# The differential-attention stage: diagonals on ScalarE, and a new order of TensorE's and VectorE's work

## What is computed

```python
def diff_attention(q, k, v, lam, lam_init, subln_g):
    # 4 heads, two maps each, head dimension 64
        s = jnp.einsum('bqhmd,bkhmd->bhmqk', q_blk, k) * scale
        s = jnp.where(mask, s, NEG_INF)
        p = jax.nn.softmax(s, axis=-1)
        att = p[:, :, 0] - lam * p[:, :, 1]
        return jnp.einsum('bhqk,bkhe->bqhe', att, v)
    ...
    o = rms_norm(o, subln_g) * (1.0 - lam_init)
```

## Time and profile before

| | |
|---|---|
| median of 3 runs | 3535.96 us (3531.65 to 3537.88) |
| the profiled execution | 3533.43 us, of which the span is 3531.3 us |
| TensorE matmul busy | 2925.1 us, 83% of the span |
| VectorE busy | 2493.0 us, 71% |
| GpSimd busy | 1844.8 us, 52% |
| ScalarE busy | 843.0 us, 24% |
| granted TensorE clock, mean | 0.943 |
| moved by DMA | 1295.97 MB, 367 GB/s over the span |

### The profile page before, as it was taken

One profiled execution on the slowest core, in us unless ns is written; L12 is line 12 of the kernel. 1 busy time (PEld: TensorE's weight loads), 2 busy tenths in 40 slices (PEclk: granted clock), 3 DMA queues, 4 the chain that ended last, 5 costly groups with the idle time before them and its releaser, 6 DMA issues.

```text
span 3531.3 us, 33020 instructions
## 1 busy us (share of the span) xinstructions
PE 2925.1 (83%) x10296; PEld 1862.3 (53%) x10296; DVE 2493.0 (71%) x5300; ACT 843.0 (24%) x2407; POOL 1844.8 (52%) x1508
## 2 busy tenths in 40 slices
PE   8999688798799878787689878888789878877777
PEld 6677444366587534355477534356478444422222
DVE  1421567787887886888888876788797887754545
ACT  2320122222210122322210123322220123332223
POOL 0000144686677534577676634587577634554554
PEclk9999899999899989998799989999799999999999
DMA  4334499999999999999999999999999999999997
GB/s 163 111 108 154 152 419 420 414 368 395 335 392 409 408 401 417 421 407 409 364 398 409 409 387 409 421 382 394 360 361 409 409 417 418 416 421 422 421 421 331
DMA packets 281580, 1295.97 MB, mean 367 GB/s; under 512 B 31808, under 2 KB 32064, under 8 KB 211776
## 3 DMA queue, kind: packets, MB, share of 16 engines
q0 software_dynamic: 216576, 1073.84, 75.7%
q1 hardware_dynamic: 64544, 218.99, 16.5%
q10 hardware_dynamic: 288, 1.05, 0.1%
HBM read 1291.65 MB, written 2.10 MB: 366 GB/s over the span
## 4 chain that ended last, share of the span: by engine, by line
PE 47%; DMA 24%; DVE 13%; POOL 7%; issue 6%; ACT 3%; DVEq 0%; SPq 0%; POOLq 0%; ACTq 0%
PE bank L594 20%; DMA ring<-in_peer,eidx 18%; PE bank L847 11%; DMA work<-in_peer,eidx 6%; POOL ring L1192 5%; PE bank L798 5%; DVE ring L1225 3%; PE bank L809 3%; DVE acc L1230 2%; PE bank L669 2%; PE bank L645 1%; POOL ring L1187 1%; ACT dg L943 1%; PE bank L624 1%; PE bank L648 1%
## 5 line engine op out<-in xcount | busy, mean ns | idle before, releaser
L1225 DVE CUSTOM_DVE_ANT_0 ring<-ring,hp 128x1024 f32<-128x1024 f32 x816 | 984.0, 1221 | 303.3 <-DMA ring<-in_peer,eidx 302.4
L1192 POOL DMA_INDIRECT ring<-in_peer,eidx x808 | 986.8, 1221 | 398.0 <-issue 221.8
L847 PE MATMUL bank<-ring,dg 128*128 128x512 f32 x1784 | 837.0, 617 | 261.7 <-ACT dg L943 231.2
L1187 POOL DMA_INDIRECT ring<-in_peer,eidx x390 | 480.5, 1232 | 920.2 <-DVE eidx L1331 423.8
L594 PE MATMUL bank<-xt,panel 128*128 128x256 f32 x4096 | 922.8, 383 | 19.8 <-ACT xt L949 5.7
L594 PEld LDWEIGHTS bank<-xt,panel 128*128 128x128 f32 x4096 | 783.6, 192 | 152.7 <-issue 30.8
L847 PEld LDWEIGHTS bank<-ring,dg 128*128 128x128 f32 x1784 | 336.5, 196 | 734.9 <-issue 697.7
L1230 DVE SCALAR_TENSOR_TENSOR acc<-ring,wgt,acc 128x1024 f32<-128x1024 f32 x326 | 415.7, 1286 | 24.8 <-DMA ring<-in_peer,eidx 21.9
L847 PE MATMUL bank<-work,dg 128*128 128x512 f32 x704 | 328.7, 610 | 106.7 <-ACT dg L943 100.5
L1225 DVE CUSTOM_DVE_ANT_0 work<-work,hp 128x1024 f32<-128x1024 f32 x208 | 252.6, 1222 | 121.6 <-DMA work<-in_peer,eidx 121.4
L1187 POOL DMA_INDIRECT work<-in_peer,eidx x154 | 195.5, 1269 | 232.9 <-PE bank L847 151.9
(11 more groups left out here) (180 smaller groups left out, 2467.8 us busy)
## 6 DMA issues: line engine op xcount, KB each, us to landing
panel<-in_panels SPq DMA_DIRECT2D x368, 512.0 KB, 6.8
ring<-in_peer,eidx POOLq DMA_INDIRECT x1198, 17.0
work<-in_rel_bias SPq DMA_DIRECT2D x16, 512.0 KB, 8.0
work<-in_peer,eidx POOLq DMA_INDIRECT x306, 22.0
gb<-in_ln_g SPq DMA_DIRECT2D x8, 512.0 KB, 8.4
gb<-in_ln_b SPq DMA_DIRECT2D x8, 512.0 KB, 10.5
panel<-in_keys SPq DMA_DIRECT2D x16, 256.0 KB, 6.4
work<-in_x SPq DMA_DIRECT2D x4, 512.0 KB, 4.6
```

Of the source, the lines that this page charges most:

```text
L847: ins = mm(pa[t * 2 + half][:, :], dg[:, i % DIAGS, :], v_row[:, half * 512:(half + 1) * 512], start=(n == group[0]), stop=(n == group[-1]))
L1187: pool.indirect_dma_start(slots(slot, 2), None, t_in["peer"], bass.IndirectOffsetOnAxis(ap=eidx[:, 0, t, c:c + 1], axis=0)).then_inc(row_i ...
L1192: pool.indirect_dma_start(slots(slot, 1), None, one_row, bass.IndirectOffsetOnAxis(ap=eidx[:, which, t, c:c + 1], axis=0)).then_inc(row_in ...
L1225: v.tensor_tensor_reduce(row, row, hp[:, t, :], 1.0, 0.0, ALU.mult, ALU.add, hid[:, t, c:c + 1]).then_inc(used, 1)
```

## The change

TensorE's order in C becomes, for each u: scores(u+1), project_qk(u+2), weigh(u), outputs(u), swap_qk(u+2).

VectorE's becomes: maxima(u), rope(u+1), the two rows of key 4, and `inverses(u)`: only the reciprocals, and for map 1 their product with minus lambda, counted by a new semaphore `c_inv`. The diagonals of C are built by ScalarE, in `weights_c(u)`: four copies of the identity with the inverse as scale. In ScalarE's queue weights_c(u) and then take_qk(u+2) stand ahead of take_weighed(u), and exponentials 2 and 3 of u+1 follow take_out(u) together. Stage A keeps its order and its diagonals on VectorE.

```diff
--- before.py
+++ after.py
@@ -435,6 +435,7 @@
         pair_wgt = sem("pair_wgt")
         smax = {k: sem(f"smax_{k}") for k in "AC"}
         dg_done = {k: sem(f"dg_done_{k}") for k in "AC"}
+        c_inv = sem("c_inv")
         rope_done = sem("rope_done")
         rms_dg = sem("rms_dg")
         lam_sums = sem("lam_sums")
@@ -755,12 +756,13 @@
                 scores("C", s, 0)
                 swap_qk(s, 1)
                 for u in range(UNITS):
-                    weigh("C", s, u)
                     if u + 1 < UNITS:
                         scores("C", s, u + 1)
+                    if u + 2 < UNITS:
+                        project_qk("C", s, u + 2)
+                    weigh("C", s, u)
                     outputs("C", s, u)
                     if u + 2 < UNITS:
-                        project_qk("C", s, u + 2)
                         swap_qk(s, u + 2)
                 pe.wait_ge(pt_ev["C"], fills_before(s, "C", UNITS))
                 pe.wait_ge(o_ev["C"], (s + 1) * UNITS)
@@ -980,6 +982,15 @@
                        accum_out=esum[:, u % 2, i:i + 1]).then_inc(e_done[kind], 1)
                     gelus((s, kind, u, i))
 
+            def weights_c(s, u):
+
+                n = s * UNITS + u
+                for m in range(2):
+                    act.wait_ge(c_inv, n * 2 + m + 1)
+                    for i in (2 * m, 2 * m + 1):
+                        fn(dg[:, u % 2 * 4 + i, :], ident, ACT.Copy, scale=rinv[:, u % 2, i:i + 1]
+                           ).then_inc(dg_done["C"], 1)
+
             def take_weighed(kind, s, u):
                 for f, (m, lo, hi) in enumerate(fills(s, kind)):
                     c = fills_before(s, kind, u) + f
@@ -1064,17 +1075,16 @@
                 take_v("C", s)
                 exps("C", s, 0)
                 for u in range(UNITS):
+                    weights_c(s, u)
+                    if u + 2 < UNITS:
+                        take_qk("C", s, u + 2)
                     take_weighed("C", s, u)
                     gelus((s, "C", u, 4))
                     if u + 1 < UNITS:
                         exps("C", s, u + 1, (0, 1))
                     take_out("C", s, u)
                     if u + 1 < UNITS:
-                        exps("C", s, u + 1, (2,))
-                    if u + 2 < UNITS:
-                        take_qk("C", s, u + 2)
-                    if u + 1 < UNITS:
-                        exps("C", s, u + 1, (3,))
+                        exps("C", s, u + 1, (2, 3))
                 act.wait_ge(o_ev["C"], (s + 1) * UNITS)
                 fn(oroot[:], osq[:], ACT.Sqrt, bias=cst[:, C_EPS2:C_EPS2 + 1], scale=1.0 / P).then_inc(rms_root, 1)
                 gelus((s, "R", 0, 0))
@@ -1507,19 +1517,28 @@
                                     ).then_inc(smax[kind], 1)
                     rows((s, kind, u, i))
 
-            def diagonals(kind, s, u):
+            def diagonals(s, u):
                 n = s * UNITS + u
                 for m in range(2):
-                    dve.wait_ge(e_done[kind], n * 4 + m * 2 + 2)
+                    dve.wait_ge(e_done["A"], n * 4 + m * 2 + 2)
                     v.reciprocal(rinv[:, u % 2, 2 * m:2 * m + 2], esum[:, u % 2, 2 * m:2 * m + 2]).then_inc(*own.one())
                     step()
                     for i in (2 * m, 2 * m + 1):
-                        if kind == "C" and m == 1:
-                            ts(dg[:, u % 2 * 4 + i, :], ident, rinv[:, u % 2, i:i + 1], small[:, 13:14],
-                               ALU.mult, ALU.mult).then_inc(dg_done[kind], 1)
-                        else:
-                            ts(dg[:, u % 2 * 4 + i, :], ident, rinv[:, u % 2, i:i + 1], None, ALU.mult
-                               ).then_inc(dg_done[kind], 1)
+                        ts(dg[:, u % 2 * 4 + i, :], ident, rinv[:, u % 2, i:i + 1], None, ALU.mult
+                           ).then_inc(dg_done["A"], 1)
+
+            def inverses(s, u):
+
+                n = s * UNITS + u
+                for m in range(2):
+                    part = rinv[:, u % 2, 2 * m:2 * m + 2]
+                    dve.wait_ge(e_done["C"], n * 4 + m * 2 + 2)
+                    ins = v.reciprocal(part, esum[:, u % 2, 2 * m:2 * m + 2])
+                    if m:
+                        ins.then_inc(*own.one())
+                        step()
+                        ins = ts(part, part, small[:, 13:14], None, ALU.mult)
+                    ins.then_inc(c_inv, 1)
 
             def attention_stage(kind, s):
                 if kind == "C":
@@ -1528,10 +1547,13 @@
                     rows((s, "A", -1, 0))
                 for u in range(UNITS):
                     maxima(kind, s, u)
-                    diagonals(kind, s, u)
-                    if kind == "C" and u + 1 < UNITS:
+                    if kind == "A":
+                        diagonals(s, u)
+                    elif u + 1 < UNITS:
                         rope(s, u + 1)
                     rows((s, kind, u, 4))
+                    if kind == "C":
+                        inverses(s, u)
 
             def rms(s):
                 rows((s, "R", 0, 0))
```

## The result

The changed kernel takes 3587.78 us (median of 5 runs, 3582.71 to 3590.06) against 3533.3 us for the kernel before (median of 5 runs by then): a ratio of 1.0152 with a 95% interval of 1.0134 to 1.017, 54 us slower. The forecast was 3556, with a range that ended at 3574. The direction was right and the size was not: 54 us instead of 20.

A forecast was written before the change was run, and what follows sets the result against it. Stage C was taken to be paced by TensorE with short waits. Its phases summed to +22.8 us, about +20 after what comes back, so 3553 for the profiled execution and 3556 for the median, range 3543 to 3574.

The forecast's parts named there:

- The waits: Full units of C: outputs waits 0.57 us for ScalarE's copy, swap 1.04 for take_out, scores 1.58 for the rotation.
- The table load ahead of the exponentials: Once per stage C in phases 1 to 3, after a gelu: +1.2 us in phase 2, +0.8 in 1 and 3.
- The sum without the clock: Stage C's changes without a clock fall in middle units: +4.9, +6.1, +5.7, +6.1 us by phase, together +22.8.
- the restart at the lower clock: Scores(1) of C in phases 1 and 3 runs slow after TensorE's long wait for VectorE: +2.8 us, up to 6.
- The rotation right behind the maxima: Scores(1) of C no longer waits for diagonals and weighing(0): 1.4, 5.4, 2.2 and 5.4 us earlier by phase.
- Diagonals on ScalarE: Most lie under projection and scores; only C's last unit could show the move, by about 0.1 to 0.5 us a phase.
- The last unit: C's last weighing comes 9.7 us behind scores(3) in phase 0 (+2.5) and 18.3 in phases 1 and 3 (+3.9).
- What comes back behind C: Gathers in flight land sooner and the DMA-bound search starts with less to do: 1 us back in each of phases 1 to 3.
- rival (a): TensorE's clock falls in C's new gaps, slowing scores and projection eight times: +25 to +45 us, typical 3586; chance 0.12.
- (b): Delays of phases 1 to 3 vanish at the DMA-bound search stretch, only phase 0's +4.9 us stays: 3541; chance 0.14.
- (c): DMA paces C too and VectorE, relieved of diagonals, frees slots sooner; new waits cost nothing in phases 1 to 3: 3525; chance 0.08.
- (d): C's swap and rotation gaps are half hidden, 1 us a unit less: 3548, within the forecast's own 0.66.

The follow-up runs named there:

- The kernel with the waits filled: The changed kernel with unread matmuls put into TensorE's new waits (behind and ahead of the swap, behind outputs(2)): 3560.23 us, ratio 1.0072 to the kernel before.
- the kernel with its last rows moved: The kernel before, with the eight rows among VectorE's maxima of C's last unit moved behind the diagonals: 3558.33 us against 3535.38, ratio 1.0074.

## Why the prediction was wrong

**The waits: right.** 0.57, 1.04 and 1.58 us were read off the last unit and the rotation of the kernel before, and 0.57, 1.08 and 1.58 came. That the same dependencies, laid bare, cost what they cost at the place where they were already bare is the part of the method that held. The table load ahead of the exponentials cost 0.63 in phases 1 and 3 (1.71 instead of 1.08) and 1.09 in phase 2, where 0.8 and 1.2 were taken.

**The sum without the clock: near, with one term too small.** The kernel with the waits filled is the measurement of this sum, since its middle units ran at 1.00. Its stages C are 5.1, 9.4, 3.7 and 9.2 us longer than before, 27.4 in sum, against 4.9, 6.1, 5.7 and 6.1, 22.8. Phases 1 and 3 miss by over 3 each, and phase 2, 2.0 less than predicted, hides part of that in the sum. In phases 1 and 3 I took 2.8 us for the restart at the lower clock, because the weighing of before had run slow for 6 us. In phase 1 of the changed kernel the whole of scores(1) ran slow, 9.92 us from start to start instead of 5.39, and the projection took 7.98 instead of 6.91: 5.6 us, near the upper end of 6 that I had named. With the waits filled these two took 9.42 and 9.27, 6.4 us more than at full clock.

**The rotation right behind the maxima: right.** Scores(0) to scores(1) in phase 1 went from 21.5 us (901.56 to 923.07) to 16.1 (916.49 to 932.60), 5.4 less, as predicted. Most of that is TensorE's order, which no longer has weighing(0) in front: the order alone gives 17.4 (923.20 to 940.63), 4.1 less. The rotation's place and the diagonals give the other 1.3.

**Diagonals on ScalarE: right.** Taken as 0.1 to 0.5 us at the last unit; alone they made no difference. The rule of the Trainium skill (page "ScalarE: Activation LUTs", section "Rules for kernel authors") that multiplications belong on VectorE would have spoken against it. The trace agrees for the single instruction, 393 ns for ScalarE's copy and 284 for VectorE's multiply in stage A, and in the time of the kernel no difference showed.

**The last unit: right.** 9.7 us predicted in phase 0 and 18.3 in phases 1 and 3; in the kernel with the waits filled 9.94 (200.44 to 210.38) and 18.13 (974.78 to 992.91). In the changed kernel itself, part of it at the lower clock, 12.83 (208.61 to 221.44) and 19.31 (987.07 to 1006.38). With two rows no longer ahead of the inverses, 1.9 to 2.4 us less.

**What comes back behind C: the right sign.** 3 us were taken, 6.2 came, in the profiled executions.

**The clock: wrong, and this is the step that failed.** The sum has no term for a lower clock in the middle units; it was put at nothing and left to rival (a), which had the mechanism and gave 3586 for all eight units. I gave it 0.12 because of one row: from 201.7 to 208.6 TensorE was busy 2.57 of 6.90 us at clock 1.00, sparser than the new gap, though by little (0.37 against 2.1 of 5.3, 0.40). That row shows that the clock did not fall in one stretch, once, ahead of a projection of 7 us. I read it as if it priced eight stretches of another shape, which come again every 17 us. Nor was it a safe row: with the diagonals alone on ScalarE the same stretch had a wait of 3.07 us instead of 2.73, and the weighing behind it took 2.90 us instead of 1.58. In the changed kernel the scores behind the gap ran slow in all eight: 6.71 and 4.97 us in phase 0, 5.52 to 6.71 in phase 2 instead of the 3.83 of full clock, and 8.41 to 9.19 in phases 1 and 3 instead of 5.55. The effect is 27 us with the restarts left as they are, half of the whole change, and the range should have reached it.

The stages C add up: 22.8 us predicted, 4.6 more with the waits filled, and 28.5 more when they are not, which is the measured 55.8 but for rounding. Those 28.5 lie in the phases as 12.8, 4.9, 6.0 and 4.8, not evenly as (a) would have it. In phase 0 scores(1) and the last unit ran slow too, which (a) did not count. In phases 1 and 3 VectorE hid a part: in phase 1 weighing(2) ended 4.7 us later behind scores(3), the last weighing began 1.2 later. And its "eight times" fits its +25 to +45 only if the projection counts four times, 26 to 44; by its words it would be 30 to 52. So that (a)'s 3586 lies 2 us from the measured 3588 is in part luck; its mechanism is what the filling showed.

The page "TensorE: Matmul & The Clock Gate" of the Trainium skill, section "A second HAM failure mode: psum-queue depth-cycling", tells of a kernel, with bf16 matmuls and PSUM banks taken in turn, in which TensorE "micro-idles between MM groups frequently enough that HAM oscillates" (HAM is its name for what sets the clock). It gives no time for it. By this the mechanism to expect would have been that of rival (a). The trace agrees: waits of 0.57, 1.08 and 1.58 us, and a granted clock of 0.77.

**(b), (c) and (d)** fell: the delays went through but for 6.2 us, the new waits cost their time in phases 1 to 3 too, so DMA did not set the pace in C, and the gaps were not hidden.

## What to carry to other kernels

Before a step is moved, list what each pair of neighbours in the new order hands over through another engine, and look for a place in the trace where the same handover stands uncovered: that row is the price, and here it held to 0.04 us. A PSUM bank that two neighbours share turns into a wait as soon as they become neighbours; another bank, with the swap moved ahead of the outputs, took back some 45 of 54 us.

Waits that are each short can lower TensorE's clock for the work around them, as here with 0.57, 1.08 and 1.58 us. One quiet row at full clock does not exclude that; where a new order thins TensorE's work in every unit, give the clock's price the same weight as the waits', and test it by filling the waits with unread matmuls.

## What the runs showed of the hardware that I had not expected

The granted clock fell in units whose longest wait was 1.58 us: 0.77 in the changed kernel, 1.00 with the same waits filled. It also differed between kernels that ran the same instructions in the same order with the same waits: 1.00 in phase 0 of the kernel before, 0.90 in the same unit of the kernel with its last rows moved. These are single executions. The mean clock of the kernel before itself ran from 0.936 to 0.945 over its executions, so whether the kernel or the execution made the difference isn't shown. Either way, one profiled execution at 1.00 doesn't show that an order keeps the clock.

A 128x512 fp32 matmul call took 0.87 us (48 records in 20.76 us for 24 calls, at a granted clock of 1.00): two records, not the length of one.
